# A hybrid decoder layer on one core: the scores of a pair of units move behind the value products and the page batch of an even slot

## Chip, core and metric

The kernel runs on one core of one Trainium2 chip. The metric is the device time of one execution in microseconds (us). The executions of the kernel before agree to about 0.9%.

## What is computed

One layer of a decoder step: a prompt of 1024 tokens (`x_prompt`), and eight sequences with one new token each and 4096 cached positions in pages of 128 rows. Both go through an input projection, a gated short convolution, stick-breaking attention (8 heads of 64) and an output projection. The attention has no softmax. Its weights come from sums of log terms that run from the last key to the first:

```python
def _stick_breaking(q, k, v, b_sb, q_pos, k_pos):
    z = jnp.einsum('bqhd,bkhd->bhqk', q, k).astype(jnp.float32) * (HEAD_DIM ** -0.5)
    z = z + b_sb.astype(jnp.float32)[None, :, None, None]
    mask = k_pos[None, :] < q_pos[:, None]
    log_keep = jnp.where(mask, jax.nn.log_sigmoid(-z), 0.0)
    after = lax.cumsum(log_keep, axis=3, reverse=True) - log_keep
    a = jnp.where(mask, jnp.exp(jax.nn.log_sigmoid(z) + after), 0.0)
    return jnp.einsum('bhqk,bkhd->bqhd', a.astype(v.dtype), v)

p = h @ w_in                      # 1032 tokens x 4096 columns, contraction 1024
o_prompt = _stick_breaking(q, k, v, ...)              # 1024 x 1024, causal
o_sample = _stick_breaking(q, pool_k[page_table], pool_v[page_table], ...)
m = jnp.concatenate([ya, yb], axis=-1) @ w_out
```

## The kernel before

Each engine has an in-order program, and semaphores join them. After a prologue (modulation, norm, transposes of the input) the work goes through **four groups** (`GROUPS`), each of two heads and 128 columns of each of the eight projected parts. The first group is written out, the other three are passes of a loop with the same body. After them comes the output projection.

A group has 34 **slots** t = 0 to 33 on TensorE. In slots 0 to 7 it projects queries, keys and values. From slot 8 on it interleaves three streams, and the order is written by hand:

- the prompt's attention, in 24 **units** u = 0 to 23 (`NU`), one per slot from slot 8 (u = t - 8). A unit is one head of one block of 128 queries against one to four key blocks (`UNITS`). A unit is two matmuls' worth of scores, a chain on VectorE and ScalarE, a transpose back on TensorE, an exponential and a product with the values. In an even slot, `scores(u)` computes the **pair** u and u+1; `outputs(u-4)` makes the value products of units u-4 and u-3; in every slot `turn(u-1)` transposes the log weights of unit u-1.
- the projection of the other five parts (`project`), half a projection in each slot, cut around `turn`: one weight tile ahead of `turn` and one behind it in even slots (`KS[0]`), four ahead and two behind in odd slots (`KS[1]`).
- the sampled sequences' values: `page_values(t)` multiplies a **batch** of four cached pages (`value_quad`, tile `ring`) with the weights `apad` in slots 1, 3, 5, 7, 8, 10, 12, 14 (sequence 2g-1, not in the first group) and 22, 24, 26, 28, 30, 31, 32, 33 (sequence 2g). It waits on the pages' DMA (`v_full`).

The chain of unit u between scores and transposes, in the order of the engines: VectorE `clamp(u)` (L947, `zc<-ps`; the pair's two clamps stand together, behind `log_weights(u-1)`), ScalarE's three activations (`rise`, `sp`, `ps`), VectorE's `reduce_pair` of the cached keys (L937), the scan (L961, `ps<-rise`), in some units a carry (L965), and the subtraction (L967, `zc<-zc,ps`), which signals `lw_ready`. `turn(u)` (L1247, `ps<-ident,zc`) waits on that. For an even unit u, scores(u) are in slot u+8 and turn(u) is in slot u+9, one slot later. `scores(u)` waits on `a_ready` of unit u-2, since there are three score banks; `outputs(u-4)` waits on `a_ready` of unit u-3. SyncE issues the page loads in an order of its own, each behind `prod_ready` (GpSimd, keys) or `v_used` (TensorE, values).

In the profile all matmuls made by the helper `mm` have line L1089. A float32 matmul has two records there, so "x16" is eight matmuls. `ps<-kT,qT` are scores, `ps<-ident_b,unseen` their causal mask, `ps<-av,vN` value products, `ps<-ring,apad` a batch of pages, `ps<-hT,wsl` the projection.

Of the kernel before, what the change touches and what calls it, by code (L numbers as in the profile page):

```python
# [72 lines left out]
NU = len(UNITS)  # L73
# [17 lines left out]
def quad_of(slot):  # L91

    for parity, slots in ((1, (1, 3, 5, 7, 8, 10, 12, 14)), (0, (22, 24, 26, 28, 30, 31, 32, 33))):
        if slot in slots:
            return parity, slots.index(slot)
    return 0, None


def stick_breaking_mixer(nc, x_prompt, x_sample, c_prompt, c_sample, cache_k, cache_v, state_conv,
# [4 lines left out]
    with ctx:  # L104
# [982 lines left out]
        def _(pe):  # L1087
            def mm(out, l, r, start, stop):
                return nc.tensor.matmul(out, l, r, start=start, stop=stop, skip_group_check=True)  # L1089
# [75 lines left out]
            def body(g, first, last_):  # L1165
                def project(m, part, chunk, ks=range(KT)):

                    if first and part == Q_:
                        pe.wait_ge(h_ready, 1 + KT * (chunk + 1))
                    if ks[0] == 0:  # L1170
                        if chunk == 0:
                            pe.wait_ge(w_full[part % 2], 16 * (4 * g + part // 2 + 1))
                        if not (first and m < 2):
                            pe.wait_ge(pj_free, PJ * g + m - 1)
                    for k in ks:
                        last = mm(ps[:, PJB + m % 2, 0:CH], wsl[:, part % 2, k, :], hT[:, k, CH * chunk:CH * (chunk + 1)],
                                  k == 0, k == KT - 1)
                    if ks[-1] == KT - 1:
                        last.then_inc(pj_full, 1)
# [33 lines left out]
                def page_values(t):  # L1213
                    parity, quad = quad_of(t)
                    if quad is None or (first and parity == 1):
                        return
                    value_quad(2 * g - parity, quad)
# [5 lines left out]
                def scores(u):  # L1223

                    t, b0, nb, _ = UNITS[u]
                    if u == 0:
                        pe.wait_ge(pj_free, PJ * g + 6)
                    if not (first and u < 2):
                        pe.wait_ge(a_ready, NU * g + u - 1)
                    diagonal = b0 + nb - 1 == t  # L1230
                    for h in range(2):
                        rows_ = slice(HD * h, HD * (h + 1))
                        z = mm(ps[:, Z + (u + h) % 3, 0:P * nb], qT[rows_, P * t:P * (t + 1)],
                               kT[rows_, P * b0:P * (b0 + nb)], True, False)
                        if not diagonal:
                            z.then_inc(z_full, 1)
                    if diagonal:
                        for h in range(2):
                            mm(ps[:, Z + (u + h) % 3, P * (nb - 1):P * nb], unseen[:, :], ident_b[:, :], False, False)\
                                .then_inc(z_full, 1)  # L1240

                def turn(u):

                    lo, nb = first_col(u), UNITS[u][2]
                    pe.wait_ge(lw_ready, NU * g + u + 1)
                    for j in range(nb):
                        last = nc.tensor.transpose(ps[:, Z + u % 3, P * j:P * (j + 1)],  # L1247
                                                   zc[:, u % 3, lo + P * j:lo + P * (j + 1)], ident[:, :])
                    last.then_inc(lwT_full, 1)

                def outputs(u):

                    t, b0, nb, _ = UNITS[u]
                    pe.wait_ge(a_ready, NU * g + u + 2)
                    if u == 0:
                        pe.wait_ge(pj_free, PJ * g + 8)
                        if not first:
                            pe.wait_ge(ob_ready, g)
                    if u == 8:
                        pe.wait_ge(o_free, g + 1)  # L1260
                    cols = slice(P * (t % 4), P * (t % 4 + 1))
                    for j in range(nb):
                        for h in range(2):
                            o = mm(ps[HD * h:HD * (h + 1), OB, cols], vN[:, b0 + j, HD * h:HD * (h + 1)],
                                   av[:, (u + h) % 4, P * j:P * (j + 1)],
                                   j == 0 and (t < 4 or b0 > 0), j == nb - 1 and b0 == 0)
                            if j == nb - 1:
                                o.then_inc(pv_done, 1)
# [25 lines left out]
                values(8)  # L1294
                for t in range(8, SLOTS + 2):
                    u = t - 8
                    if u < NU and u % 2 == 0:
                        scores(u)
                    if u % 2 == 0 and u >= 4:
                        outputs(u - 4)  # L1300
                    page_values(t)
                    if u < NU:
                        m, ks = 9 + u // 2, KS[u % 2]
                    else:
                        m, ks = 21 + u - NU, (range(0, 4), range(4, KT))
                    project(m, GC_ + (m - 9) // 3, (m - 9) % 3, ks[0])
                    if 1 <= u <= NU:
                        turn(u - 1)
                    project(m, GC_ + (m - 9) // 3, (m - 9) % 3, ks[1])
                    if t == 19:  # L1310
                        cumulate(0)
                    if t in (8, 9, 10):
                        key_rows(t - 8)
                    if first and t == 9:
                        gate_strips(1)
                    if first and t == 12:
                        gate_sums(1)
                    if t == 12:
                        spread_q(1)
                    if t == 17 and not first:  # L1320
                        own_heads_T(1)
# [5 lines left out]
            def value_quad(seq, quad):  # L1327

                if quad == 0:
                    pe.wait_ge(d_a, seq + 1)  # L1330
                    if not (isinstance(seq, int) and seq == 0):
                        pe.wait_ge(d_free, seq)
                for rr in (2 * quad, 2 * quad + 1):
                    pe.wait_ge(v_full[rr % 4], v_fill(seq, rr))
                for j in range(4):
                    rr = 2 * quad + j // 2
                    last = mm(ps[32 * j:32 * j + NH, DB, :], apad[:, :, 4 * quad + j], vring[:, rr % 4, j % 2, :],
                              quad == 0, quad == NQUAD - 1)
                last.then_inc(v_used, 1)
# [4 lines left out]
            def heads_T(seq):  # L1344
                for c in range(GROUPS):
                    last = mm(ps[:, DB, c:c + 1], om[:, P * c:P * (c + 1)], ones[:, 0:1], True, True)
                last.then_inc(d_oT, 1)

            run_groups(pe, body)

            def conv_rows():
# [105 lines left out]
```

## Time and profile before

| | us |
|---|---|
| median of 3 runs | 928.25 (923.77 to 932.14) |
| the profiled execution | 924.33 |
| its span, first to last instruction | 922.6 |
| mean granted TensorE clock | 0.983 of full speed |

The profile shows one execution. Its time lies 1.73 us above its span and 3.92 us below the median. Starts and durations are microseconds from the start of the span; groups of the kernel begin at about 57, 234, 415 and 597 us, and slot 8 of them at 104.6, 283.5, 464.5 and 645.5 us.

### The profile page before, as it was taken

To read this page: it belongs to the slowest core of one execution; us is meant where nothing else is said; L and a number is where in the kernel's file an instruction comes from. 1 tells how busy PE (TensorE), PEld (TensorE's weight loads), DVE (VectorE), ACT (ScalarE), POOL (GpSimd) and SP (SyncE) were. 2 spreads that over 40 slices of the span, in tenths; PEclk is the share of its full clock that TensorE was granted. 3 is DMA by queue.
4 is the path that set the end of the run, shared out by engine and by line. 5 is a ranking of instruction groups with operands and counts; after the bars stand their busy time and mean duration, and the time that the engine had idled before them with its cause. 6 is when DMAs were issued, how large, how long until landed. Compare 5 with 4: busy or idle time off the path is not lost.

```text
span 922.6 us, 15515 instructions
## 1 busy us (share of the span) xinstructions
PE 843.5 (91%) x4281; PEld 492.2 (53%) x4281; DVE 553.4 (60%) x772; ACT 330.4 (36%) x641; POOL 328.8 (36%) x154
## 2 busy tenths in 40 slices
PE   0899987999999979999998899999978999999996
PEld 0557644555676545565855555558535555434442
DVE  2543598985435899844268998432768984232335
ACT  6311255652202646512036564110454641021112
POOL 0006455551175446502645564044534640100000
PEclk9989999999999999999999999999999999899999
DMA  8976634667378866763888676637866677474101
GB/s 325 340 253 230 215 127 158 231 228 243 100 239 251 277 194 210 237 201 111 250 269 256 196 240 212 211 103 237 279 198 203 215 229 256 167 231 137 70 23 48
DMA packets 128052, 189.14 MB, mean 205 GB/s; under 512 B 9680, under 2 KB 50685, under 8 KB 127952
## 3 DMA queue, kind: packets, MB, share of 16 engines
q1 hardware_dynamic: 96752, 172.27, 56.4%
q10 hardware_dynamic: 31200, 15.73, 6.0%
q8 instruction: 39, 0.64, 0.3%
q14 instruction: 61, 0.50, 0.2%
HBM read 179.49 MB, written 8.49 MB: 204 GB/s over the span
## 4 chain that ended last, share of the span: by engine, by line
PE 63%; SPq 14%; DVE 9%; issue 8%; DMA 3%; ACT 1%; POOL 1%; DVEq 0%; POOLq 0%; ACTq 0%
PE ps L1089 58%; SPq L343 6%; SPq L351 6%; PE ps L1247 3%; DVE ps L961 2%; DMA ring<-in_cache_v_dram 2%; DVE zc L967 1%; PE ps L1130 1%; DMA pages<-in_page_table_dram 1%; POOL prod L488 1%; SPq L311 1%; DVE zb L819 1%; DVE zc L947 1%; DVE zx L832 1%; DMA hT<-in_w_out_dram 1%
## 5 line engine op out<-in xcount | busy, mean ns | idle before, releaser
L488 POOL TENSOR_TENSOR prod<-ring,qb 128x1024 f32<-128x1024 f32 x128 | 316.3, 2479 | 413.9 <-DVE zd L937 184.8
L1089 PE MATMUL ps<-hT,wsl 128*128 128x344 f32 x1344 | 430.1, 461 | 4.1 <-issue 4.1
L1089 PEld LDWEIGHTS ps<-hT,wsl 128*128 128x128 f32 x1344 | 243.2, 192 | 157.5 <-issue 47.7
L937 DVE TENSOR_REDUCE zd<-prod 128x16 f32<-128x1024 f32 x128 | 155.2, 1212 | 41.2 <-POOL prod L488 40.8
L947 DVE TENSOR_SCALAR zc<-ps,bsb 128x512 f32<-128x512 f32 (+3 forms) x96 | 55.2, 612 | 74.7 <-PE ps L1089 74.4
L511 ACT ACTIVATE rise<-ps,bsh 128x512 f32<-128x512 f32 (+3 forms) x96 | 55.5, 579 | 73.2 <-DVE zc L947 72.8
L511 ACT ACTIVATE av<-ps 128x512 f32<-128x512 f32 (+3 forms) x96 | 46.7, 487 | 91.3 <-PE ps L1247 90.7
L1089 PE MATMUL ps<-ring,apad 128*8 128x512 f32 x512 | 69.5, 615 | 9.1 <-DMA ring<-in_cache_v_dram 9.1
L1247 PE MATMUL ps<-ident,zc 128*128 128x128 f32 x288 | 49.1, 280 | 29.3 <-DVE zc L967 29.3
L1089 PE MATMUL ps<-hT,xy 128*128 128x512 f32 x160 | 73.1, 601 | 0.8 <-DMA hT<-in_w_out_dram 0.8
L961 DVE TENSOR_TENSOR_SCAN ps<-rise,ps 128x512 f32<-128x512 f32 (+3 forms) x64 | 65.5, 1023 | 10.6 <-ACT ps L511 9.7
L1247 PEld LDWEIGHTS ps<-ident,zc 128*128 128x128 f32 x288 | 36.5, 143 | 56.8 <-DVE zc L967 39.2
L1089 PEld LDWEIGHTS ps<-wsl,hT 128*128 128x128 f32 (+1 forms) x576 | 63.4, 181 | 6.4 <-issue 5.0
L1089 PE MATMUL ps<-wsl,hT 128*128 128x128 f32 (+1 forms) x576 | 65.9, 275 | 0.0
L967 DVE TENSOR_TENSOR zc<-zc,ps 128x512 f32<-128x512 f32 (+3 forms) x96 | 52.9, 551 | 2.2
L1089 PEld LDWEIGHTS ps<-hT,xy 128*128 128x128 f32 x160 | 30.5, 193 | 41.7 <-issue 39.2
L511 ACT ACTIVATE sp<-zc 128x512 f32<-128x512 f32 (+3 forms) x96 | 49.6, 517 | 0.0
L511 ACT ACTIVATE ps<-sp 128x512 f32<-128x512 f32 (+3 forms) x96 | 47.5, 495 | 3.0
L1089 PE MATMUL ps<-kT,qT 64*128 64x512 f32 (+3 forms) x192 | 44.0, 535 | 0.0
L1089 PE MATMUL ps<-av,vN 128*64 128x128 f32 x576 | 42.0, 281 | 0.0
L1089 PEld LDWEIGHTS ps<-av,vN 128*64 128x64 f32 x576 | 30.5, 136 | 13.3 <-issue 8.5
L504 POOL TENSOR_TENSOR rs<-ss,half 128x1 f32<-128x1 f32 x8 | 4.3, 544 | 91.6 <-DVE ss L1073 91.6
(215 smaller groups left out, 645.3 us busy)
## 6 DMA issues: line engine op xcount, KB each, us to landing
ring<-in_cache_k_dram SPq DMA_DIRECT2D x256, 256.0 KB, 3.0
ring<-in_cache_v_dram SPq DMA_DIRECT2D x256, 256.0 KB, 2.9
wsl<-in_w_in_dram ACTq DMA_DIRECT2D x30, 512.0 KB, 5.4
ring<-in_w_ada_dram SPq DMA_DIRECT2D x6, 2048.0 KB, 11.1
xy<-in_x_prompt_dram SPq DMA_DIRECT2D x2, 2048.0 KB, 10.3
out_dram<-oT SPq DMA_DIRECT2D x8, 512.0 KB, 3.7
ring<-in_x_prompt_dram SPq DMA_DIRECT2D x8, 512.0 KB, 6.6
hT<-in_w_out_dram SPq DMA_DIRECT2D x5, 512.0 KB, 6.0
```

The lines of the kernel that those rows point to most:

```text
L311: sp_e.dma_start(xs, x_sample.rearrange("b l d -> (b l) d")).then_inc(small_in, 16)
L343: _, numbers = nc.values_load_multi_w_load_instructions(pages[0:1, bass.ds(seq * PAGES + (PAGES - 2 - r), 2)], engines=[mybir.EngineType.S ...
L351: sp_e.dma_start(dst[:, j, :], src).then_inc(full, 16)
L488: pool.tensor_tensor(prod[:, t % 2].rearrange("p (j c) -> p j c", j=2), kring[:, t % 4], qb[:, t // 16].unsqueeze(1).to_broadcast([P, 2, H ...
L511: nc.scalar.activation(out, in_, func, **kw).then_inc(done, 1)
L819: lk(v.tensor_tensor(zb[:, :].rearrange("p (h r) -> p h r", h=NH), zd[:, k], bsb[:, :].unsqueeze(2).to_broadcast([P, NH, PAGES]), ALU.add))
L937: v.tensor_reduce(zd[:, t // 16, :, r:r + 2], prod[:, t % 2].rearrange("p (j h d) -> p h j d", j=2, h=NH), AX_X, ALU.add)\
L947: v.tensor_scalar(zc[:, u % 3, lo:QC], ps[:, Z + u % 3, 0:QC - lo], bsb[:, bass.ds(2 * g + h, 1)], CLAMP, ALU.add, ALU.min).then_inc(zc_re ...
L961: v.tensor_tensor_scan(back(sums), back(rise[:, par_, lo + 1:QC + 1]), back(sums), start, ALU.add, ALU.add).then_inc(scan_done, 1)
L967: v.tensor_tensor(zc[:, u % 3, lo:QC], zc[:, u % 3, lo:QC], sums, ALU.subtract)\
L1089: return nc.tensor.matmul(out, l, r, start=start, stop=stop, skip_group_check=True)
L1247: last = nc.tensor.transpose(ps[:, Z + u % 3, P * j:P * (j + 1)], zc[:, u % 3, lo + P * j:lo + P * (j + 1)], ident[:, :])
```

## The change

In the loop over slots 8 to 33 on TensorE, the call of `scores(u)` in even slots stands behind `outputs(u-4)` and `page_values(t)`, no longer ahead of them. Nothing is added or taken away, and no other engine's program changes. The waits inside the three functions move with them.

```diff
@@ -1294,11 +1294,11 @@
                 values(8)
                 for t in range(8, SLOTS + 2):
                     u = t - 8
-                    if u < NU and u % 2 == 0:
-                        scores(u)
                     if u % 2 == 0 and u >= 4:
                         outputs(u - 4)
                     page_values(t)
+                    if u < NU and u % 2 == 0:
+                        scores(u)
                     if u < NU:
                         m, ks = 9 + u // 2, KS[u % 2]
                     else:
```

On TensorE, slot 28 (unit 20) of the written-out group stands like this before, from the end of slot 27 to the transposes of unit 20 in slot 29 (here one row counts matmuls, not records):

```order
L1089 MATMUL ps<-hT,wsl 128x344 x2
L1089 MATMUL ps<-kT,qT 128x512 x2
L1089 MATMUL ps<-ident_b,unseen 128x128 x2
L1089 MATMUL ps<-av,vN 64x128 x8
L1089 MATMUL ps<-ring,apad 8x512 x4
L1089 MATMUL ps<-hT,wsl 128x344
L1247 MATMUL ps<-ident,zc 128x128 x3
L1089 MATMUL ps<-hT,wsl 128x344 x5
L1247 MATMUL ps<-ident,zc 128x128 x4
```

and like this in the changed kernel:

```order
L1089 MATMUL ps<-hT,wsl 128x344 x2
L1089 MATMUL ps<-av,vN 64x128 x8
L1089 MATMUL ps<-ring,apad 8x512 x4
L1089 MATMUL ps<-kT,qT 128x512 x2
L1089 MATMUL ps<-ident_b,unseen 128x128 x2
L1089 MATMUL ps<-hT,wsl 128x344
L1247 MATMUL ps<-ident,zc 128x128 x3
L1089 MATMUL ps<-hT,wsl 128x344 x5
L1247 MATMUL ps<-ident,zc 128x128 x4
```

The last row is unit 20's transposes. Twelve matmuls that stood between the scores and it now stand ahead of the scores.

On TensorE, slot 12 (unit 4) of the looped groups before, with the instructions that wait (L1229 is the wait of `scores`, L1254 and L1256 those of `outputs`, L1334 those on the pages' DMA):

```order
L1089 MATMUL ps<-hT,wsl 128x344 x2
L1229 ISA
L1089 MATMUL ps<-kT,qT 128x384 x2
L1089 MATMUL ps<-ident_b,unseen 128x128 x2
L1254 ISA
L1256 ISA
L1089 MATMUL ps<-av,vN 64x128 x2
L1334 ISA x2
L1089 MATMUL ps<-ring,apad 8x512 x4
L1174 ISA
L1089 MATMUL ps<-hT,wsl 128x344
```

and in the changed kernel:

```order
L1089 MATMUL ps<-hT,wsl 128x344 x2
L1254 ISA
L1256 ISA
L1089 MATMUL ps<-av,vN 64x128 x2
L1334 ISA x2
L1089 MATMUL ps<-ring,apad 8x512 x4
L1229 ISA
L1089 MATMUL ps<-kT,qT 128x384 x2
L1089 MATMUL ps<-ident_b,unseen 128x128 x2
L1174 ISA
L1089 MATMUL ps<-hT,wsl 128x344
```

The wait on the pages' DMA (L1334) now stands in front of the scores.

## Rows read from the trace of the kernel before

**Rows 1.** The page's part 1: busy time, share of the span, instructions.

```profile
PE 843.5 (91%) x4281; PEld 492.2 (53%) x4281; DVE 553.4 (60%) x772; ACT 330.4 (36%) x641; POOL 328.8 (36%) x154
```

**Rows 2.** Waits: who waited for whom: us in total, times, longest us.

```profile
PE ps L1247 <- DVE zc L967: 29.3, 17, 2.9
PE ps L1089 <- DMA ring<-in_cache_v_dram: 9.1, 6, 4.5
...
DVE zc L947 <- PE ps L1089: 74.4, 27, 14.0
```

**Rows 3.** Timeline of TensorE, second group, slots 28 and 29: start, duration, what, records.

```profile
373.42 1.13 PE L1089 MATMUL ps<-kT,qT 64*128 64x512 f32 x4
...
374.70 1.09 PE L1089 MATMUL ps<-av,vN 128*64 128x128 f32 x16
375.73 1.06 PE L1089 MATMUL ps<-ring,apad 128*8 128x512 f32 x8
376.72 0.85 PE L1089 MATMUL ps<-hT,wsl 128*128 128x344 f32 x2
...
380.62 0.60 PE L1247 MATMUL ps<-ident,zc 128*128 128x128 f32 x4
```

**Rows 4.** Timeline of VectorE, the same slots: clamps and log weights of unit 20.

```profile
374.98 1.41 DVE L947 TENSOR_SCALAR zc<-ps,bsb 128x512 f32<-128x512 f32 x2 [0.96 <-PE ps L1089]
...
379.21 0.68 DVE L967 TENSOR_TENSOR zc<-zc,ps 128x512 f32<-128x512 f32 x1
```

**Rows 5.** Timeline of TensorE, second group: slot 25, scores of slot 26, slots 27, 31.

```profile
363.72 0.60 PE L1247 MATMUL ps<-ident,zc 128*128 128x128 f32 x4
...
365.41 0.92 PE L1089 MATMUL ps<-kT,qT 64*128 64x384 f32 x4
...
371.84 0.49 PE L1247 MATMUL ps<-ident,zc 128*128 128x128 f32 x3
...
390.36 0.60 PE L1247 MATMUL ps<-ident,zc 128*128 128x128 f32 x4
```

**Rows 6.** Timeline of VectorE, second group: units 16, 18 (clamps, log weights), 22.

```profile
362.42 0.68 DVE L967 TENSOR_TENSOR zc<-zc,ps 128x512 f32<-128x512 f32 x1
...
367.27 1.14 DVE L947 TENSOR_SCALAR zc<-ps,bsb 128x384 f32<-128x384 f32 x2
...
370.82 0.55 DVE L967 TENSOR_TENSOR zc<-zc,ps 128x384 f32<-128x384 f32 x1
...
387.96 0.69 DVE L967 TENSOR_TENSOR zc<-zc,ps 128x512 f32<-128x512 f32 x1
```

**Rows 7.** Timeline of TensorE, second group, slots 12 to 17.

```profile
298.06 0.92 PE L1089 MATMUL ps<-kT,qT 64*128 64x384 f32 x4
...
299.12 0.44 PE L1089 MATMUL ps<-av,vN 128*64 128x128 f32 x4
...
300.37 1.06 PE L1089 MATMUL ps<-ring,apad 128*8 128x512 f32 x8 [0.81 <-DMA ring<-in_cache_v_dram]
...
310.26 1.06 PE L1089 MATMUL ps<-ring,apad 128*8 128x512 f32 x8 [0.73 <-DMA ring<-in_cache_v_dram]
...
315.15 0.60 PE L1247 MATMUL ps<-ident,zc 128*128 128x128 f32 x4
...
318.12 0.88 PE L1089 MATMUL ps<-av,vN 128*64 128x128 f32 x12
...
326.01 0.66 PE L1247 MATMUL ps<-ident,zc 128*128 128x128 f32 x4 [2.92 <-DVE zc L967]
```

**Rows 8.** Timeline of VectorE, second group: log weights of units 6, 8, clamps of 12.

```profile
313.25 0.69 DVE L967 TENSOR_TENSOR zc<-zc,ps 128x512 f32<-128x512 f32 x1
...
325.28 0.68 DVE L967 TENSOR_TENSOR zc<-zc,ps 128x512 f32<-128x512 f32 x1
...
342.44 1.41 DVE L947 TENSOR_SCALAR zc<-ps,bsb 128x512 f32<-128x512 f32 x2
```

**Rows 9.** Windows of TensorE, fourth group, after a wait: us, busy, granted clock, DMA.

```profile
676.00:680.00 4.00, 4.00 (x17) 0.57 0.70 244
```

## The prediction

> **What bounds the kernel.** I read the shares of the page first: TensorE is busy for 91% of the span, the next engine for 60% [rows 1]. What delays TensorE delays the end. So I went to the waits. TensorE's two largest inside the groups are the transposes of a unit's log weights, which wait for VectorE's subtraction (29.3 us in 17 waits), and the batches of cached pages, which wait for their DMA (9.1 us in 6) [rows 2]. The reader should also see there that VectorE waits for TensorE ahead of its clamps (74.4 us in 27): in these places the chain of a unit starts when its scores arrive, and whatever delays the scores delays the chain. The question is then, slot by slot, how much earlier than needed the log weights are ready. That is in the timelines of both engines.
>
> **The change, part by part.** Nothing is added: the same matmuls run, at the same durations. The scores of an even slot start later by what now stands ahead of them. In slot 28 that is the value products, from 374.70 to 375.73, 1.03 us, and the batch, from 375.73 to 376.72, 0.99 us [rows 3]: a **move of 2.02 us**. The chain follows: VectorE waits 0.96 us for these scores and starts its clamps at 374.98, 0.28 us behind their end at 374.70 [rows 3, 4], and the subtraction ends at 379.21 + 0.68 = 379.89. The transposes start at 380.62 [rows 3]. Where they do wait, they start 0.05 us behind the subtraction (326.01 against 325.28 + 0.68 = 325.96) [rows 7, 8]. So slot 28 has a **spare** of 380.62 - 379.89 - 0.05 = 0.68 us. A move beyond the spare becomes idle time of TensorE: 2.02 - 0.68 = 1.34 us. TensorE cannot fill it, since its queue is in order and what stood in front of the transposes has already run ahead of the scores.
>
> The other even slots with scores, in the second group:
> - Slot 24 (unit 16): move 2.02, subtraction ends at 362.42 + 0.68 = 363.10, transposes at 363.72 [rows 5, 6], spare 0.57, new wait **1.45**.
> - Slot 26 (unit 18): the value products are half as many, about 0.55 us by [rows 3], so the move is 1.54. TensorE comes 1.45 late. The scores would start 2.99 late. Before, they started at 365.41 and took about 0.84 of the 0.92 us shown, and the clamps came at 367.27, with no wait shown [rows 5, 6]: 1.02 behind their end, 0.8 more than the 0.2 that the engine needs. So the clamps come 2.2 late, the subtraction (ends 371.37) too, and the transposes, at 371.84 with a spare of 0.42, have 1.45 + 0.42 = 1.87 to meet it: wait **0.33**.
> - Slot 28: **1.34**, as above. VectorE's lateness of 2.2 does not matter there, since it idled 0.96 us ahead of the clamps and the scores come 1.45 + 0.33 + 2.02 = 3.80 late.
> - Slot 30 (unit 22): move 0.80 + 0.99 = 1.79, with the twelve-record value products at the 0.80 us worked out below; a second batch stands ahead of the transposes: 390.36 against 387.96 + 0.69 [rows 5, 6], spare 1.66, wait **0.13**.
> - Slots 18, 20 and 22 (units 10, 12, 14): nothing. VectorE is late there for reasons of its own. Unit 12's clamps start at 342.44 with no wait for their scores [rows 8], and the transposes' waits come from that queue, which the move doesn't lengthen. Slots 8 and 10 have moves of 0.99, within the spares.
>
> The late stretch (slots 22 to 33) sums to 1.45 + 0.33 + 1.34 + 0.13 = **3.25 us a group**, and its rows repeat in all four groups to 0.05 us: **13.0 us**. Beyond it VectorE is some 1.5 us further behind than TensorE; it idles for several us at the end of a group, so that costs nothing.
>
> In the early stretch two batches wait for the pages' DMA. SyncE's issue decides when these land, not TensorE, so the batches stay where they are in time and the scores now come behind them, where they had run during the wait. Slot 12: the scores and mask take 299.12 - 298.06 = 1.06 us, and the batch starts at 300.37 after a wait of 0.81 [rows 7]. TensorE ends **1.06** later. Slot 14: the batch starts at 310.26 after a wait of 0.73 [rows 7]; coming 1.06 late, but without the scores, TensorE is still there before that, so the scores with mask (374.70 - 373.42 = 1.28 us [rows 3]) now come behind it: TensorE is 1.28 late in all, 0.22 more. These scores start at 310.26 + 0.99 = 311.25. They had started at 307.59 (318.12 - 1.28 is the like start two slots on, at 316.84), so they are 3.66 late; the subtraction ended at 313.25 + 0.69 = 313.94 [rows 8] and now ends at 317.60; the transposes, at 315.15 + 1.28 = 316.43 [rows 7], wait **1.22** with the 0.05. Slot 16 (unit 8): no batch, and the transposes already wait 2.92 [rows 7]. The twelve-record value products (0.88 shown, 0.80 to the next start) go into the wait in full: **0.80**. The early stretch of the second group: 1.28 + 1.22 + 0.80 = 3.3 us. In the third and fourth the page waits fall otherwise (the 4.5 us wait [rows 2] is the fourth's slot 14, where the scores had run ahead of it); the same working gives 3.1 and 2.9. In the first group no batch stands in these slots: 0.6 + 0.8 = 1.4. Together **10.7 us**.
>
> The clock: a stretch behind the 4.5 us wait ran at a granted clock of 0.57 over 4 us [rows 9], mostly the lower level, 1.2 GHz; the loss is 0.43 x 4 = 1.7 us. The 2.92 us wait of the second group left its four transposes at 0.66 us, against 0.60 elsewhere [rows 3, 7]: no fall. With that wait at 3.7 and new ones of 1.2 to 2 before it, I add one such stretch, **1.7 us**; the bounds are 0 and two in every group, 8 x 1.7 = 13.6.
>
> Sum: 13.0 + 10.7 + 1.7 = **25.4 us**. Against the profiled execution, 924.33 + 25.4 = 949.7; against the median of the runs, 3.92 above it, 953.6. I take **952**. Executions differ by some 0.9%, so 1% is about what a measurement can tell from no change.
>
> **Rivals.**
> (a) The clock falls in every group. For it: the longer waits, 3.7 us in slot 17 and 2 us of page wait in slot 12. Against it: 2.92 us went by without a fall. Time: 952 + 13.6 - 1.7 = 964.
> The Trainium skill (TensorE: Matmul & The Clock Gate, "HAM oscillation — how this bites in real kernels") says that waits between batches of matmuls let the clock fall again, so that the work behind each starts slow. By that rule the time is that of (a); the trace agrees for the 4.5 us wait and not for the 2.92 us one.
> (b) Part of the cost is given back. The spares are read from one execution, and the modelled ends of matmuls may be off by 0.3 us. The chain may also pass more quickly when its neighbours on VectorE and ScalarE stand elsewhere. If half of each wait goes, the sum is about 12: 938 to 940.
> (c) Not slower. VectorE's own queue, not the scores, decides when a chain starts, as in units 10 and 12, and the scores' later start falls into time in which it is busy; meanwhile each batch runs 1.06 to 1.28 us earlier within its slot, frees its buffers and sends the next load off earlier, so that the page waits of slots 12 and 14 (7.9 of the 9.1 us) shrink. Price: 0 for the chains and up to -7.9, so 920 to 928. It decides where VectorE reaches a clamp more than 2.0 us behind its scores. At slot 28 it is 0.28 us [rows 3, 4], at slot 26 1.0, and only at slot 20 enough.
> (d) The change doesn't do what it says. Excluded: the new order of instructions shows it in every even slot.
>
> **How the numbers follow.** The forecast has 0.62 (940 to 960), (a) 0.17, (b) 0.13, (c) 0.08, split into 0.04 faster by over 1% and 0.04 within 1%. (b)'s lower end adds 0.01 to within 1%. The range runs from 938, (b) with the median's own spread, to 966, (a) with it. Faster 0.04, same 0.05, slower 0.91.
>
> **What would show it.** TensorE's wait for the subtraction grows from 29.3 to about 49 us (13.0 from the late stretch, some 7 from the early one), with new waits of 1.3 to 1.5 us in slots 25 and 29, one of 1.2 in slot 15, and 3.7 in slot 17. In slots 12 and 14 the page waits grow by about the scores, 1.1 and, where the batch is still late, up to 0.2. The sum of the busy times stays. The four groups each last 5 to 7 us longer, and the prologue and the output projection do not. I would be wrong if the waits in slots 25 and 29 were under 0.5 us, if the chain from clamp to subtraction (379.89 - 374.98 = 4.9 us) came out shorter, or if the page waits vanished.

## The result, and the profile after

The changed kernel takes 956.23 us (median of 4 runs, 951.92 to 957.56) where the kernel before takes 930.19 us on the same chip (4 runs, 923.77 to 935.72). The ratio is 1.0251, with a 95% interval of 1.0197 to 1.0305: slower by 2.5%, 26 us. The profiled execution took 955.51 us. Executions more than 1.5% above the fastest of the same kernel, all of them at a low granted clock, are left out of the ratios below, which matters for e3 alone: the median of all its twelve executions is 1.4% above that of the kernel before.

The profile page of the changed kernel, span, busy time of each engine (its share of the span, its instructions) and the row of granted clocks:

```profile
span 953.8 us, 15515 instructions
## 1 busy us (share of the span) xinstructions
PE 852.6 (89%) x4281; PEld 491.5 (52%) x4281; DVE 551.8 (58%) x772; ACT 327.6 (34%) x641; POOL 329.2 (35%) x154
...
PEclk9989999999999999999999999999999999999999
```

Against [rows 1], TensorE runs the same 4281 matmuls but is busy 9.1 us longer. That is the same work at a lower clock in places, as the windows below bear out: the same scores, value products and batches take 1.13, 1.09 and 1.06 us in both kernels where the clock is full. The rest of the 31.2 us by which the profiled spans differ is waiting. The view of waits of the changed kernel (engine, tile, line, releaser: idle us, number of waits, longest):

```profile
PE ps L1247 <- DVE zc L967: 46.1, 31, 3.9
PE ps L1089 <- DMA ring<-in_cache_v_dram: 16.3, 10, 4.4
...
DVE zc L947 <- PE ps L1089: 121.1, 39, 14.9
```

Against [rows 2], the transposes wait 16.8 us more, in 31 places instead of 17, and the batches of cached pages 7.2 us more. VectorE waits for TensorE's scores 46.7 us more ahead of its clamps. It is not VectorE that has become slow. With the 9.1 us of busy time the growth sums to 33.1 us, some 2 more than the span's, which other idle time gives back.

The timeline of TensorE in the late stretch of the second group, slots 24 to 29 (start, duration, what ran, and in brackets the idle time before it), answers to [rows 3, 5]:

```profile
371.50 1.13 PE L1089 MATMUL ps<-kT,qT 64*128 64x512 f32 x4
...
378.03 0.66 PE L1247 MATMUL ps<-ident,zc 128*128 128x128 f32 x4 [1.44 <-DVE zc L967]
...
386.67 0.55 PE L1247 MATMUL ps<-ident,zc 128*128 128x128 f32 x3 [0.30 <-DVE zc L967]
...
388.31 1.09 PE L1089 MATMUL ps<-av,vN 128*64 128x128 f32 x16
389.33 1.06 PE L1089 MATMUL ps<-ring,apad 128*8 128x512 f32 x8
390.32 1.13 PE L1089 MATMUL ps<-kT,qT 64*128 64x512 f32 x4
...
396.84 0.66 PE L1247 MATMUL ps<-ident,zc 128*128 128x128 f32 x4 [1.32 <-DVE zc L967]
```

The value products and the batch now stand in front of the scores of slot 28, 2.01 us of them. The waits of slots 25, 27 and 29 are 1.44, 0.30 and 1.32 us, where the forecast had 1.45, 0.33 and 1.34. VectorE's part of it, unit 20, answers to [rows 4]:

```profile
391.87 1.41 DVE L947 TENSOR_SCALAR zc<-ps,bsb 128x512 f32<-128x512 f32 x2 [2.60 <-PE ps L1089]
...
396.11 0.68 DVE L967 TENSOR_TENSOR zc<-zc,ps 128x512 f32<-128x512 f32 x1
```

From the clamps' start to the subtraction's end it is 396.11 + 0.68 - 391.87 = 4.92 us, as before (4.91). Only its start has moved, and VectorE's wait ahead of it has grown from 0.96 to 2.60 us.

The early stretch of the same group on TensorE, slots 10 to 18, answers to [rows 7]:

```profile
297.32 1.06 PE L1089 MATMUL ps<-ring,apad 128*8 128x512 f32 x8 [1.20 <-DMA ring<-in_cache_v_dram]
...
304.76 1.06 PE L1089 MATMUL ps<-ring,apad 128*8 128x512 f32 x8
...
317.96 1.90 PE L1089 MATMUL ps<-ring,apad 128*8 128x512 f32 x8 [4.40 <-DMA ring<-in_cache_v_dram]
319.79 1.79 PE L1089 MATMUL ps<-kT,qT 64*128 64x512 f32 x4
...
326.85 0.66 PE L1247 MATMUL ps<-ident,zc 128*128 128x128 f32 x4 [1.19 <-DVE zc L967]
...
338.57 1.11 PE L1247 MATMUL ps<-ident,zc 128*128 128x128 f32 x4 [3.85 <-DVE zc L967]
...
345.63 0.66 PE L1247 MATMUL ps<-ident,zc 128*128 128x128 f32 x4 [0.74 <-DVE zc L967]
```

Slot 15 waits 1.19 us (forecast 1.22) and slot 17 3.85 (3.7). The page waits do not stand where the forecast had them: one of 1.20 us in slot 10, none in slot 12, 4.40 in slot 14. Behind the longest waits the durations are long: the batch takes 1.90 us instead of 1.06, the scores 1.79 instead of 1.13, four transposes 1.11 instead of 0.66. The windows of these places (from:to, us, busy, granted clock, DMA share, GB/s) say why:

```profile
318.00:321.00 3.00, 3.00 (x12) 0.50 0.93 261
338.00:342.00 4.00, 3.43 (x12) 0.57 0.22 80
528.00:532.00 4.00, 2.60 (x7) 0.67 0.35 135
720.00:724.00 4.00, 3.70 (x13) 0.57 0.19 71
150.00:154.00 4.00, 3.46 (x10) 0.57 0.28 93
```

0.50 is the lower level of the clock, 1.2 GHz; 0.57 over 4 us is mostly that level. The last four windows stand behind slot 17 of the second, third, fourth and first group. In the kernel before, TensorE waited 2.92 us there in the second group and its clock stayed full, but in the fourth group of the same trace it fell behind a wait of the same length. Slot 18 of the second group, then slots 17 and 18 of the fourth, and the window behind that slot 17:

```profile
332.77 0.66 PE L1247 MATMUL ps<-ident,zc 128*128 128x128 f32 x4 [1.94 <-DVE zc L967]
...
692.87 0.86 PE L1247 MATMUL ps<-ident,zc 128*128 128x128 f32 x4 [2.92 <-DVE zc L967]
...
699.88 0.66 PE L1247 MATMUL ps<-ident,zc 128*128 128x128 f32 x4 [0.52 <-DVE zc L967]
```

```profile
693.00:697.00 4.00, 4.00 (x16) 0.57 0.06 22
```

Summing the clock that is missing over 2 us windows from 100 to 820 us, the kernel before lost 8.5 us in 4 stretches and the changed one 15.3 us in 9 (6.8 us of it in the four behind slot 17).

### The profile page after: what moved, and what is told of

It reads as the page before. It is cut to its first block, busy times and chain, and to the rows that moved or that the text cites. A ratio compares the mean times of both kernels' runs of the same rounds, so it can differ in the third digit from the quotient of the medians.

```text
span 953.8 us, 15515 instructions
## 1 busy us (share of the span) xinstructions
PE 852.6 (89%) x4281; PEld 491.5 (52%) x4281; DVE 551.8 (58%) x772; ACT 327.6 (34%) x641; POOL 329.2 (35%) x154
## 4 chain that ended last, share of the span: by engine, by line
PE 56%; SPq 14%; DVE 11%; issue 8%; DMA 5%; ACT 4%; POOL 1%; DVEq 0%; POOLq 0%; ACTq 0%
PE ps L1089 53%; SPq L351 6%; SPq L343 6%; DVE ps L961 4%; PE ps L1247 3%; DMA ring<-in_w_ada_dram 2%; DVE zc L967 2%; DVE zc L947 2%; DMA ring<-in_cache_v_dram 2%; ACT ps L511 1%; ACT sp L511 1%; POOL prod L488 1%; SPq L311 1%; DVE zx L832 1%; DVE zb L819 1%
## 5 line engine op out<-in xcount | busy, mean ns | idle before, releaser
L1247 PE MATMUL ps<-ident,zc 128*128 128x128 f32 x288 | 50.9, 287 | 46.2 <-DVE zc L967 46.1
L1089 PE MATMUL ps<-ring,apad 128*8 128x512 f32 x512 | 71.6, 629 | 16.3 <-DMA ring<-in_cache_v_dram 16.3
L1089 PE MATMUL ps<-kT,qT 64*128 64x512 f32 (+3 forms) x192 | 46.7, 565 | 0.0
## 6 DMA issues: line engine op xcount, KB each, us to landing
ring<-in_w_ada_dram SPq DMA_DIRECT2D x6, 2048.0 KB, 10.7
xy<-in_x_prompt_dram SPq DMA_DIRECT2D x2, 2048.0 KB, 10.9
```

## The experiments

The theories. **A**, the forecast: scores that start later than the spare allows delay the chain, and TensorE idles for the rest. **B**: the batches of pages, which no longer have the scores in their wait, carry the cost. **C**: the same matmuls cost more in their new surroundings, without the waits. All were timed in five rounds against the kernel before. Waits and busy times are of the profiled execution, in us; "transposes" is TensorE's wait for the log weights, "pages" that for the batches' DMA.

| kernel | ratio (95%) | transposes | pages | PE busy | span |
|---|---|---|---|---|---|
| before | 1 | 29.3 | 9.1 | 843.5 | 922.6 |
| after | 1.0251 (1.0197 to 1.0305) | 46.1 | 16.3 | 852.6 | 953.8 |
| e1 | 1.0105 (1.0057 to 1.0154) | 32.8 | 16.5 | 851.6 | 941.3 |
| e2 | 1.0062 (1.0028 to 1.0096) | 26.6 | 12.7 | 849.4 | 929.4 |
| e3 | 1.0090 (1.0039 to 1.0140) | 36.6 | 10.9 | 850.0 | 939.7 |
| e4 | 1.0032 (0.9995 to 1.0070) | 25.0 | 16.1 | 855.0 | 937.4 |
| e5 | 1.0141 (1.0093 to 1.0189) | 23.3 | 25.0 | 856.6 | 945.7 |
| e6 | 1.0348 (1.0300 to 1.0396) | 39.6 | 23.2 | 864.5 | 971.9 |
| e7 | 0.9917 (0.9882 to 0.9953) | 22.8 | 16.4 | 845.7 | 926.4 |
| e8 | 1.0207 (1.0154 to 1.0260) | 31.4 | 12.0 | 863.1 | 948.0 |
| e9 | 0.9830 (0.9789 to 0.9870) | 27.6 | 1.4 | 842.5 | 911.2 |
| e10 | 1.0078 (1.0048 to 1.0108) | 43.2 | 1.4 | 850.5 | 934.9 |
| e11 | 0.9759 (0.9722 to 0.9796) | 20.9 | 1.8 | 844.3 | 910.9 |
| e12 | 0.9851 (0.9811 to 0.9890) | 9.9 | 0.6 | 858.2 | 917.2 |

**e1, the value products alone ahead of the scores.** Against the changed kernel:

```
                         outputs(u - 4)
-                    page_values(t)
                     if u < NU and u % 2 == 0:
                         scores(u)
+                    page_values(t)
```

> Value products stand ahead of the scores, the page batch stays behind them. Theory A (each slot pays the move of its scores beyond the spare of its transposes): moves of 1.03, 0.55, 1.03 and 0.80 us against spares of 0.57, 0.42, 0.68 and 1.66 leave waits of 0.46 in slot 25, 0 in 27, 0.35 in 29 and 0 in 31, 3.2 us over four groups; slot 17 pays 0.80 in each group (3.2) and slot 15 of the first group 0.6. No page wait is uncovered: they stay near 9 us. Sum 7.0, ratio 1.0075. Rival B (the cost comes from the scores standing behind the pages' DMA wait and the slow clock after it): no cost, ratio 1.000. Rival C (the moved matmuls cost more in the new place by themselves): TensorE's busy time grows and the transposes' waits don't.

1.0105; the 1.0075 expected lies in the interval. In the middle groups slots 25 and 29 wait 0.30 and 0.19 us: that is what remains of a move of 1.03, the rest is spare. Slot 17, where no batch stands and the value products do, waits 3.42 to 3.87 us in the four groups, as in the changed kernel. Both follow A. The page waits were expected to stay near 9 us and are 16.5.

**e2, the batch alone ahead of the scores.**

```
                     u = t - 8
-                    if u % 2 == 0 and u >= 4:
-                        outputs(u - 4)
                     page_values(t)
                     if u < NU and u % 2 == 0:
                         scores(u)
+                    if u % 2 == 0 and u >= 4:
+                        outputs(u - 4)
```

> The page batch stands ahead of the scores, the value products stay behind them. Theory A: moves of 0.99 in slots 24, 26, 28 and 30 leave waits of 0.42, 0, 0.31 and 0: 2.9 us over four groups; in the early stretch the scores come out from under the page waits (1.1 to 1.3 us in three groups), and slot 15 waits about 1.1 in each of these; slot 17 pays nothing, since its slot 16 has no batch. With one more slow stretch of 1.7 the sum is about 11 us, ratio 1.012, and the page waits are 3 to 7 us above those of before. Rival B: nearly the whole cost, ratio 1.02 or more.

1.0062, about half of what was expected. Slots 25 and 29 wait 0.27 and 0.15 us in the middle groups. Slot 15 waits 0.28 to 0.47 us in three groups, where some 1.1 were expected: that is the miss. Slot 17, which has no batch, waits 2.91 us, as before the change. The two halves of the move thus cost 1.05% and 0.62%, 1.7% together, and both at once 2.5%: less than the whole, since the spare of a slot is used up once and not twice. The gap of 0.8% is only about as large as the noise of the three ratios, but the waits show the same: in the transposes 3.5 us more and 2.7 us less than before, and 16.8 us more with both. The remaining waits of e1 and e2 are each some 0.15 us shorter than the forecasts; this was not followed up.

**e3, the new order only from slot 22 on.**

```
                     u = t - 8
+                    if t < 22 and u % 2 == 0:
+                        scores(u)
                     if u % 2 == 0 and u >= 4:
                         outputs(u - 4)
                     page_values(t)
-                    if u < NU and u % 2 == 0:
+                    if t >= 22 and u < NU and u % 2 == 0:
                         scores(u)
```

> The new order in slots 22 to 30 alone, the order of before in slots 8 to 20. Theory A: 1.45 + 0.33 + 1.34 + 0.13 = 3.25 us a group, 13.0 in all, ratio 1.014, with waits of the transposes 13 us above before and the page waits and the clock as before. Rival B: no page wait stands in these slots, so no cost, ratio 1.000.

1.009, in the range from 1.004 to 1.014, where 1.014 was expected. The new waits, in TensorE's timeline of the second group:

```profile
370.94 0.66 PE L1247 MATMUL ps<-ident,zc 128*128 128x128 f32 x4 [1.43 <-DVE zc L967]
...
379.59 0.55 PE L1247 MATMUL ps<-ident,zc 128*128 128x128 f32 x3 [0.30 <-DVE zc L967]
...
389.76 0.66 PE L1247 MATMUL ps<-ident,zc 128*128 128x128 f32 x4 [1.32 <-DVE zc L967]
```

The third group shows 1.43, 0.31 and 1.32, but the first 1.10 and 0.99 and the last 1.25 and 1.14: 10.6 us in all, the same sum as in the changed kernel, where 13.0 was forecast. No page wait stands in the late slots, so B has nothing to say here, and the cost is there all the same. Over the whole kernel the transposes wait only 7.3 us more than before, since waits of slots 18 and 19 shrank where the clock fell behind slot 17, as the part on the prediction works out.

**e4, the chain is given more time.** In the changed kernel's order, all of an odd slot's remaining projection runs ahead of the transposes, which thus come later:

```
-KS = ((range(0, 1), range(1, 2)), (range(2, 6), range(6, 8)))
+KS = ((range(0, 1), range(1, 2)), (range(2, 8), range(8, 8)))
...
-                    project(m, GC_ + (m - 9) // 3, (m - 9) % 3, ks[1])
+                    if len(ks[1]):
+                        project(m, GC_ + (m - 9) // 3, (m - 9) % 3, ks[1])
```

> The new order, and in odd slots all six weight tiles of the projection ahead of the transposes, none behind (before: four and two). That puts 1.25 us more work between an even unit's scores and its transposes. Theory A: the waits of slots 25, 27, 29 and 31 fall from 1.45, 0.33, 1.34 and 0.13 to about 0.2, 0, 0.1 and 0, that of slot 15 goes, that of slot 17 falls by 1.25, but the scores of slot 18 may wait up to 0.5 for the exponential. What is left against before is the page exposure, 4 to 5 us: ratio 1.005. Rival B: as the new order alone, 1.02 to 1.025, since the page waits stay. Rival C: the same, since the moved matmuls cost what they cost.

1.0032, not told from no change. The transposes' wait is 25.0 us where the changed kernel has 46.1:

```profile
370.02 0.66 PE L1247 MATMUL ps<-ident,zc 128*128 128x128 f32 x4 [0.27 <-DVE zc L967]
374.27 0.66 PE L1247 MATMUL ps<-ident,zc 128*128 128x128 f32 x4 [0.40 <-DVE zc L967]
...
387.78 0.66 PE L1247 MATMUL ps<-ident,zc 128*128 128x128 f32 x4 [0.17 <-DVE zc L967]
```

The scores stand as late as in the changed kernel, and with later transposes most of the cost is gone. C falls: were the matmuls dearer by their order alone, the order would cost as much here, and where the clock is full they take the same time in either order. TensorE's busy time is higher here than in the changed kernel (855.0 against 852.6 us), but so is the clock missing in the windows (27.3 against 15.3 us). The kernel before was not run with this split, so the 1.0032 is not a pure price of the order.

**e5 and e6, half the bytes of the value pages,** in the order of before (e5) and in the new one (e6). Each value page is loaded for 64 of its 128 partitions; the other half of the products is computed from what the buffer holds.

```
-            def load_pair(dst, cache, numbers, full):
+            def load_pair(dst, cache, numbers, full, n=P):
...
-                    sp_e.dma_start(dst[:, j, :], src).then_inc(full, 16)
+                    sp_e.dma_start(dst[0:n, j, :], src[0:n, :]).then_inc(full, 16)
...
-                load_pair(vring[:, rr % 4], cache_v, numbers, v_full[rr % 4])
+                load_pair(vring[:, rr % 4], cache_v, numbers, v_full[rr % 4], P // 2)
```

> The order of before, but each load of a page of cached values brings 64 of its 128 rows (the other half of the tile keeps old data, so the sampled sequences' outputs are not the reference's). It measures the page waits alone. If these come from landing time, the waits for the pages' DMA in the groups go to about 0 and the ratio is 0.99; if they come from SyncE's issue, which stays the same in number, they stay.

> The new order with the same half loads (the sampled outputs are not the reference's). Theory A: without page waits the order costs only what the chains cost: late stretch 3.05 us in the two middle groups and 2.1 to 2.4 in the outer two (as the run of the late stretch alone showed) = 10.6, slot 15 about 1.2 in three groups and 0.65 in the first = 4.3, slot 17 0.9 each = 3.6, sum 18.5, and 1 to 2 us of slow clock: a ratio of 1.021 against the half-load kernel of before, about 1.011 against the kernel before if that one is at 0.99. Rival B (page waits and what follows them are the main cost): the two half-load kernels are within 0.5% of each other.

1.0141 and 1.0348, and the page waits grow, from 9.1 to 25.0 us in e5, where they were expected to go or to stay. The DMA issues on SyncE's queue in e5 (start, time of the issues) show the reason:

```profile
460.13 3.69 SPq L351 DMA_DIRECT2D ring<-in_cache_v_dram  x4
...
467.50 3.68 SPq L351 DMA_DIRECT2D ring<-in_cache_v_dram  x4
...
483.78 3.14 SPq L351 DMA_DIRECT2D ring<-in_cache_k_dram  x4
```

In the kernel before, four value loads take 3.11 us to issue. Half the partitions makes it 3.7, with a median of 473 ns for one issuing instruction instead of 333. From issue to landing a load takes 2.6 us instead of 2.9 (medians). So it is SyncE's issue that sets when the pages land, not the bytes. As a means against the page waits the pair failed. As a test of the order it counts: 1.0348 / 1.0141 = 1.020, so the order costs about the same where the page waits do not grow with it (25.0 and 23.2).

**e7, VectorE's queue ahead of slot 17,** in the order of before. On VectorE the preparation of the decode scores stood ahead of the log weights for which slot 17 waits. It now stands behind them:

```
+                    if u >= 1:
+                        log_weights(g, u - 1, first)
                     if t == 17:
                         v.wait_ge(red_done, 32 * g + 16)
                         decode_scores(0)
-                    if u >= 1:
-                        log_weights(g, u - 1, first)
```

> The order of before on TensorE; on VectorE the two steps that prepare the sampled sequence's scores in slot 17 (bias and clamp, 2.5 us there in the trace, with one of them at 2.2 instead of 0.4 us while GpSimd multiplies) stand behind unit 8's log weights, no longer ahead of them. It tests whether the waits of slots 17 to 21 are VectorE's queue. Theory: unit 8's transposes wait about 0.4 instead of 2.9 us, the wait of slot 18 grows by what VectorE still has to do, and the net gain is the 1.8 us in which the step stood still, in each group: 7 us, ratio 0.992. If the waits came from the scores or ScalarE, nothing changes: 1.000.

0.9917, faster than before the change. VectorE's timeline in e7:

```profile
328.11 0.68 DVE L967 TENSOR_TENSOR zc<-zc,ps 128x512 f32<-128x512 f32 x1
328.71 0.42 DVE L819 TENSOR_TENSOR zb<-zd,bsb 128x256 f32<-128x256 f32 x1
```

and TensorE's in the same kernel:

```profile
328.85 0.66 PE L1247 MATMUL ps<-ident,zc 128*128 128x128 f32 x4 [0.47 <-DVE zc L967]
...
336.26 0.66 PE L1247 MATMUL ps<-ident,zc 128*128 128x128 f32 x4 [2.59 <-DVE zc L967]
```

Slot 17's wait falls from 2.92 to 0.47 us and slot 18's rises from 1.94 to 2.59. The preparation's own addition takes 0.42 us. In its old place the kernel before shows

```profile
321.44 2.21 DVE L819 TENSOR_TENSOR zb<-zd,bsb 128x256 f32<-128x256 f32 x1
```

while GpSimd ran a product until 321.00 + 2.36 = 323.36 us. The addition ends at 323.65, 0.29 us behind GpSimd: it had been held up. The Trainium skill (SBUF — State Buffer, "Who interferes with whom") says that an operation of VectorE with two inputs in SBUF and one of GpSimd that reads SBUF contend, and that the later one is blocked for the whole of the other. These rows agree: the addition began 0.44 us behind GpSimd's product and took 2.21 us instead of 0.42.

**e8, slot 17's wait filled,** in the new order. TensorE runs seven matmuls of 512 columns, whose result nobody reads, ahead of slot 17's transposes:

```
+                def fill(n):
+                    misc_ready(M_CUM0)
+                    for _ in range(n):
+                        mm(ps[:, MB, :], ones[:, :], qsP[:, :], True, True)
...
                     project(m, GC_ + (m - 9) // 3, (m - 9) % 3, ks[0])
+                    if t == 17:
+                        fill(7)
```

> The new order with seven more 512-column matmuls (to a free bank, results not used) ahead of unit 8's transposes in slot 17, where TensorE idles for 3.4 to 3.9 us in the changed kernel; they take about 3.1 us. If the slow clock behind that wait comes from the idle time, the granted clock in the 4 us behind slot 17 stays at full speed in all groups, in place of 0.5 to 0.6 over some 3.5 us. The time: a slow stretch costs 1.7 us, of which 1.2 are taken back in the shorter wait of slot 18, so a gain of 0.5 a group against the new order, 2 us: ratio 1.023. If the clock falls for another reason, the stretches stay.

1.0207, and the filler was mis-sized: each matmul has two records, 0.43 us apart, and takes 0.86 us, so that seven take 6.0 us, more than the wait. The transposes start some 2 us later for it (11.2 us behind their scores instead of 9.2). TensorE's timeline, filler to slot 18:

```profile
332.19 6.17 PE L1089 MATMUL ps<-qsP,ones 128*128 128x512 f32 x14
338.20 0.60 PE L1252 MATMUL ps<-ident,zc 128*128 128x128 f32 x4
...
343.71 0.66 PE L1252 MATMUL ps<-ident,zc 128*128 128x128 f32 x4 [0.74 <-DVE zc L967]
```

The windows of e8 behind slot 17 in the second, third, fourth and first group:

```profile
338.00:342.00 4.00, 4.00 (x37) 1.00 0.09 7
526.00:530.00 4.00, 4.00 (x16) 1.00 0.13 48
714.00:718.00 4.00, 4.00 (x15) 1.00 0.28 109
148.00:152.00 4.00, 4.00 (x11) 1.00 0.42 131
```

The clock stays full in all of them, four transposes take 0.60 us instead of 1.11, and the clock missing over the groups falls from 15.3 to 5.1 us; 6.8 us of that stood behind slot 17. So the low clock there comes from the waiting and is part of the change's price. Whether the kernel gains by it is not shown: 1.0207 and 1.0251 are not told apart, and the filler itself is too long.

**e9 and e10, the pages in time.** SyncE reads the four page numbers of a batch of value pages from the table in one go, instead of two and two, and issues earlier. e9 has the order of before, e10 the new one.

```
-                    for rr in (2 * quad, 2 * quad + 1):
-                        load_v(2 * g - parity, rr, None if first and quad < 2 else 16 * g - 8 * parity + quad - 1)
+                    _, four = nc.values_load_multi_w_load_instructions(
+                        pages[0:1, bass.ds((2 * g - parity) * PAGES + (PAGES - 4 - 4 * quad), 4)],
+                        engines=[mybir.EngineType.SP], min_val=0, max_val=cache_k.shape[1] - 1)
+                    if not (first and quad < 2):
+                        sp_e.wait_ge(v_used, 16 * g - 8 * parity + quad - 1)
+                    for j, rr in enumerate((2 * quad, 2 * quad + 1)):
+                        load_pair(vring[:, rr % 4], cache_v, four[2 - 2 * j:4 - 2 * j], v_full[rr % 4])
```

> The order of before; SyncE reads the four page numbers of a batch of cached values in one table read in place of two, the loads themselves are the same. In the trace a read with its checks takes SyncE about 1.4 us, so its round of two slots falls from 9.0 to about 7.9 us, below TensorE's 8.9. If the page waits come from SyncE's issue, they fall from 9 to 16 us to under 4 and the ratio is 0.988. If they come from the DMA's transfer, nothing changes: 1.000.

> The new order with the same single table read. Theory A: with the page waits gone in both, the new order costs the chains' part alone, some 18.5 us and 1 to 2 of slow clock, ratio 1.020 to the same kernel in the old order, so about 1.008 to the kernel before. Rival B (the page waits and what follows them carry the cost): within 0.5% of the old order with the single read, 0.99.

0.983 and 1.0078. In both, no page wait is left inside the groups. The order still costs 1.0078 / 0.983 = 1.025, about 0.5% either way, what it cost with the page waits, where 1.020 was expected. **B falls** as the carrier of the cost. The profile page of e9, part 1:

```profile
PE 842.5 (92%) x4281; PEld 491.9 (54%) x4281; DVE 552.2 (61%) x772; ACT 329.8 (36%) x641; POOL 329.0 (36%) x154
```

its view of waits:

```profile
PE ps L1252 <- DVE zc L972: 27.6, 17, 2.9
```

part 1 of e10:

```profile
PE 850.5 (91%) x4281; PEld 495.8 (53%) x4281; DVE 550.3 (59%) x772; ACT 327.8 (35%) x641; POOL 329.3 (35%) x154
```

and the waits of e10:

```profile
PE ps L1252 <- DVE zc L972: 43.2, 29, 3.9
```

This pair is the clean reading of the change. The spans differ by 934.9 - 911.2 = 23.7 us: 15.6 in the transposes' waits and 8.0 in TensorE's busy time, and nothing is left over. The medians differ by as much, 23.6 us. From slot 8 of one group to slot 8 of the next it takes 6.4, 6.0 and 6.9 us longer.

**e11, both mends, order of before:** the edits of e7 and e9 together.

> The order of before on TensorE, the single table read on SyncE, and on VectorE the preparation of the sampled scores behind unit 8's log weights. The two act on different waits (pages in slots 8 to 14, transposes in slots 17 and 18), so they should add: 0.992 x 0.988 = 0.980.

0.9759 (909.02 us), the fastest kernel here. The two gains, 0.8% and 1.7%, add up.

**e12, e11 with a filler of five matmuls in slot 18,** where e7 had left the longest wait:

```
+                    if t == 18:
+                        fill(5)
```

> As the kernel with both mends, with five more 512-column matmuls (results not used) ahead of unit 9's transposes in slot 18, where 2.6 to 3.6 us of wait are left. They take 2.2 us. If the clock falls behind that wait, its fall goes away and up to 1.7 us a group come back: ratio 0.975; if it doesn't fall there, as often before with waits of 2.9 us, no change to the kernel without them, 0.980.

0.9851: slower than e11 by 0.9%. The expectation had taken half the real time for a filler matmul, as in e8. The transposes' waits fall from 20.9 to 9.9 us, but TensorE is busy 13.9 us longer. Five matmuls take 4.3 us, the wait they fill was 2.6 to 3.5, so the surplus of some 1 to 1.7 us a group, 4 to 7 us, is of the size of the loss (6.3 us of span). Idle time that the view of waits puts down to issue also grew, from 5.7 to 11.3 us, all of it at the seams between the looped groups; its cause is open. A filler ahead of a late chain buys no time here.

## Why the prediction was right

Time, direction and the path were as forecast: 956 us against 952, 26.0 us against 25.4. Two of its terms were mis-sized in opposite directions, and a third stays open. That the mechanism is waits beyond the spare is shown; that the sum comes within 0.6 us of the measured difference is luck.

**Spare and move, right.** Slots 25, 27 and 29 of the second group to 0.03 us, slot 15 to 0.03, slot 17 to 0.15 (3.85 against 3.7). Slot 31, with 0.13 forecast, starts 0.15 us later behind its projection than before (2.56 us against 2.41), too little for the timeline to show as a wait. The chain from clamp to subtraction kept its length. Units 10, 12 and 14 cost next to nothing, as said: their chains start by VectorE's own queue, and the waits of 0.93 and 1.73 us that stand there before are 1.07 and 1.74 after. In all, the transposes' waits grew to 46.1 us, against about 49 forecast. The groups were to last 5 to 7 us longer each. The clean pair shows that, with 6.4, 6.0 and 6.9 us for the first three; in the changed kernel it is 6.5, 10.9 and 10.8, since page waits of the second and third group grew too.

**The late stretch, too large:** 10.6 us instead of 13.0. The step that failed is "its rows repeat in all four groups to 0.05 us". This holds for TensorE's queue and not for the chain. In the first and the last group the waits were 2.07 and 2.39 us, in the middle ones 3.06 each. In the kernel before, the chain in the first group, from the clamps at 179.56 to the subtraction's end at 184.37, took 4.81 us, where [rows 4] give 4.91, and its clamps started 0.05 us behind the modelled end of the scores instead of 0.28. ScalarE's program is written out for these two groups and looped for the middle ones, and from clamp to exponential it is 0.79 us in the first group and 0.96 in the second. That the loop is the reason fits these rows, but no run tested it. One group was measured and four were charged.

**The early stretch, partly right.** Slots 15 and 17 came as worked out. Slot 13 of the first group, for which the forecast had nothing, waits 0.52 us more. And slot 18's wait shrank, from 1.94 to 0.74 us in the second group, which the forecast did not look at. It is the low clock that does this, not the later scores: in the fourth group of the kernel before and in the third of e3 slot 17 waits 2.92 us as elsewhere, but the clock falls behind it, and slot 18 waits 0.52 and 0.74 us, against 1.93 in the same two groups where it does not fall. A low stretch behind slot 17 takes TensorE 1.7 us of busy time and gives back some 1.2 of it in the next wait. So the transposes' waits outside the late stretch grew by 6.2 us and not by 7.

The page exposure, some 3.4 us of the 10.7, is open. The page waits moved to slot 10 and grew by 7.2 us, but over the kernels they go from 9.1 to 16.4 us in an unchanged early order (before, e3, e7), and with no page wait at all the order costs the same 2.5%. A term of some 4 us is not excluded: the time of all executions without their missing clock (worked out below) grew by 20 us in the changed kernel and by 15.5 in the clean pair, a difference that the scatter of the executions may also explain.

**The clock, too small.** Forecast: 1.7 us more, one stretch, and yet the same sum of busy times. Measured: 9.1 us more busy time in the profiled executions and 8.0 in the clean pair. The first figure is a high one, since the profiled execution of the kernel before had one of its highest granted clocks, 0.983. Taking (1 - mean granted clock) x span for every execution on record, the clock missing in the changed kernel is 28.1 us on average and in the kernel before 23 to 25, which is 3 to 5 us less; in the clean pair it is 23.5 and 16.3. The step that failed is "2.92 us went by without a fall". It was read in one place, and the fourth group of the same trace shows a fall behind the same wait. Behind slot 17, waits of 2.47 to 2.92 us were followed by the low clock in 9 of 16 groups (before, e2, e3, e9), and waits of 3.42 to 3.87 us in 12 of 12 (after, e1, e10). So behind slot 17 the clock fell in every group, as rival (a) had it and as the Trainium skill (TensorE: Matmul & The Clock Gate, "HAM oscillation — how this bites in real kernels") says of waits between batches of matmuls. e8 shows the cause: with TensorE kept at work there, the clock stayed up. What (a) had too dear was the sum: it charged two new stretches in every group, where the windows show nine in all instead of four.

**The rivals.** (b), half of the cost given back, is excluded by the waits of slots 25 to 29, which came in full in the middle groups; a part was given back in the outer groups and in slot 18. (c), not slower: VectorE was waiting for its scores in slots 24 and 28 (1.13 and 0.96 us in the kernel before), so it had nothing to hide them in. The profiled spans differ by 31.2 us and the medians by 26.0; the profiled execution of the kernel before was among its fastest.

## What to carry to other kernels

When work is moved ahead of the first step of a chain through another engine, take for each place the spare between the chain's result and the matmul that needs it, and charge only what the move exceeds it by; do so in every group, as the written-out and the looped ones differ. Then add what the new waits cost in clock, as a price on the same scale as the waits (8 us beside 15.6 here), look at every place of the trace with a like wait before saying that the clock holds, and test the sum with the other waits removed, in a pair of kernels that differ in nothing but the order. The larger gain lay elsewhere: in an operation of VectorE that stood ahead of the log weights and in SyncE's reading of page numbers, 2.4% together.

## What the runs showed of the hardware

- Loading 64 of the 128 partitions of a page takes SyncE longer to issue than loading all: 3.68 against 3.11 us for four loads, 473 against 333 ns for the issuing instruction.
- Reading four page numbers at once instead of two and two brings the issue of a batch's four loads from 3.11 to 1.88 us in most rows and saves 1.7% of the whole time:

```profile
471.55 1.88 SPq L351 DMA_DIRECT2D ring<-in_cache_v_dram  x4
```

- A 32-bit matmul of 512 columns, 128 by 128, took 0.86 us at the full clock, as two records 0.43 us apart.
- After waits of 3.4 to 3.9 us (12 of 12 groups; behind waits of 2.5 to 2.9 us in 9 of 16) TensorE's clock stood at its lower level for most of the next 4 us while TensorE worked (0.57 over 4 us), and in e4 for some 10 us on end, with TensorE busy for 10.2 of 12 us:

```profile
330.00:342.00 12.00, 10.20 (x44) 0.58 0.40 132
```
